# A decoder layer on one core: the front and the projection over blocks of 416 tokens, and two thirds of the modulation made in the mixer

## The reference, cut to what matters

```python
mod = (silu(c) @ w_ada + b_ada)            # 6 x 1024 columns: shift_m, scale_m, gate_m, shift_f, scale_f, gate_f
h = rmsnorm(x, g_pre_mix) * (1 + scale_m) + shift_m
proj = h @ w_in                            # 1536 conv columns, 512 z, 4 b, 4 a, 512 q, 128 k, 128 v
xconv = silu(sum(xp[:, i:i + t] * conv_w[i] for i in range(4)))     # causal, over the 1536 conv columns
o_a = gated delta rule over q, k, v of xconv, chunks of the prompt, state carried; normed, times silu(z)
o_b = sliding-window attention over q_b, k_b, v_b with sinks
x = x + gate_m * rmsnorm(concat(o_a, o_b) @ w_o, g_post_mix)
h = rmsnorm(x, g_pre_ffn) * (1 + scale_f) + shift_f
x = x + gate_f * rmsnorm(square(relu(h @ w_up)) @ w_down, g_post_ffn)
```

## Time and profile before

| | us |
|---|---|
| median of 3 runs (3320.49 to 3322.53) | 3320.68 |
| the profiled execution | 3326.54 |
| its span in the profile | 3324.7 |
| TensorE busy in the span | 3082.3 (93%) |
| VectorE busy | 1573.7 (47%) |
| ScalarE busy | 906.7 (27%) |
| GpSimd busy | 424.6 (13%) |

### The profile page before, as it was taken

The page is one execution under the profiler, slowest core; times in us unless marked ns, Lnnn a source line. Parts: engine busy times, 40 slices in busy tenths (PEclk is TensorE's granted clock), DMA queues, the critical chain, the costliest instruction groups (busy, mean ns, idle before and its releaser), DMA issues. The chain is left out here.

```text
span 3324.7 us, 53221 instructions
## 1 busy us (share of the span) xinstructions
PE 3082.3 (93%) x20508; PEld 2771.5 (83%) x20508; DVE 1573.7 (47%) x2062; ACT 906.7 (27%) x1675; POOL 424.6 (13%) x573
## 2 busy tenths in 40 slices
PE   6799999978999999778987999999998999999996
PEld 2399999977888888767877889988997899999995
DVE  1373655724555555534543444344445444444444
ACT  2332333332333333312333111111212212122121
POOL 2011111112333333100110000000003100000003
PEclk9899999987999999957998999999999999999998
DMA  6643434340111121133544101111114311111112
GB/s 228 220 123 116 137 113 138 114 134 22 50 53 50 53 59 50 41 88 115 179 139 118 51 25 50 50 44 32 50 51 138 94 45 31 50 50 50 50 51 101
DMA packets 320081, 278.92 MB, mean 84 GB/s; under 512 B 13402, under 2 KB 291135, under 8 KB 319960
## 3 DMA queue, kind: packets, MB, share of 16 engines
q1 hardware_dynamic: 312408, 252.58, 25.7%
q0 software_dynamic: 7568, 24.91, 2.0%
HBM read 216.23 MB, written 62.16 MB: 84 GB/s over the span
## 5 line engine op out<-in xcount | busy, mean ns | idle before, releaser
L81 PE MATMUL up_ps<-h_hi,w_up_hi 128*128 128x264 f32 (+1 forms) x2048 | 580.5, 283 | 20.0 <-DVE h_lo L2523 13.2
L82 PE MATMUL up_ps<-h_lo,w_up_hi 128*128 128x264 f32 (+1 forms) x2048 | 583.2, 285 | 0.0
L83 PE MATMUL up_ps<-h_hi,w_up_lo 128*128 128x264 f32 (+1 forms) x2048 | 580.5, 283 | 0.0
L2545 DVE TENSOR_TENSOR y<-y,down_ps 128x1024 f32<-128x1024 f32 (+1 forms) x272 | 332.0, 1220 | 316.0 <-PE down_ps L83 315.4
L81 PE MATMUL down_ps<-w_down_hi,u_hi 128*128 128x512 f32 x1088 | 433.5, 398 | 17.3 <-issue 9.2
L83 PE MATMUL down_ps<-w_down_hi,u_lo 128*128 128x512 f32 x1088 | 429.6, 395 | 0.0
L82 PE MATMUL down_ps<-w_down_lo,u_hi 128*128 128x512 f32 x1088 | 428.0, 393 | 0.0
L81 PEld LDWEIGHTS up_ps<-h_hi,w_up_hi 128*128 128x128 f32 x2048 | 389.2, 190 | 22.7 <-issue 14.5
L81 PE MATMUL proj_ps<-h_hi,w_in_hi 128*128 128x262 f32 x1408 | 400.9, 285 | 0.0
L82 PE MATMUL proj_ps<-h_lo,w_in_hi 128*128 128x262 f32 x1408 | 400.2, 284 | 0.0
L83 PE MATMUL proj_ps<-h_hi,w_in_lo 128*128 128x262 f32 x1408 | 399.3, 284 | 0.0
(11 more groups left out here) (437 smaller groups left out, 4856.3 us busy)
## 6 DMA issues: line engine op xcount, KB each, us to landing
w_in_raw<-in_w_in SPq DMA_DIRECT2D x91, 512.0 KB, 3.9
w_up_raw<-in_w_up SPq DMA_DIRECT2D x66, 512.0 KB
w_down_raw<-in_w_down SPq DMA_DIRECT2D x64, 512.0 KB, 4.6
w_ada_cols<-in_w_ada SPq DMA_DIRECT2D x16, 1536.0 KB, 7.0
proj_scratch<-chunk_out POOLq DMA_DIRECT2D x88, 256.0 KB, 3.3
qkv<-proj_scratch SPq DMA_DIRECT2D x16, 768.0 KB, 5.0
x_tile<-in_x_prompt SPq DMA_DIRECT2D x16, 512.0 KB
mixed_T<-mixed_scratch SPq DMA_DIRECT2D x16, 512.0 KB, 4.4
```

What stands on the lines that cost most here:

```text
L81: nc.tensor.matmul(out, whi, mhi, start=first, stop=False)
L82: nc.tensor.matmul(out, whi, mlo, start=False, stop=False)
L83: return nc.tensor.matmul(out, wlo, mhi, start=False, stop=last)
L2545: v.tensor_tensor(acc, acc, pd[r, (par * H.tiles + t) % 2], ALU.add).then_inc(H.s_y, 1)
```

## The change

The modulation stage makes only the first 2048 of the 6144 columns (shift_m and scale_m): their weights are loaded row-wise, whole, during `constants` (8 DMAs of 1 MB), and TensorE takes them as stationary weights (128x128, unsplit float32) with `scT` as the 9 moving columns, 128 products into one accumulator. During `constants` the first 416 rows of x and the first three chunks of w_in are loaded too. `xnT` is gone.

The projection goes over 5 blocks of 416 tokens (the last one holds 384 of the prompt and the 32 samples), so each product is 416 columns wide and a chunk is 24 products. It norms and turns the next block's x itself: the loads on SyncE, the square on ScalarE, the power on GpSimd, four transposes per k-slice on TensorE after the chunks 12 to 19, and the modulation on VectorE straight from PSUM. The block's left neighbours for the convolution are kept as 3 columns per chunk (`chunk_tails`) instead of being computed again. The first tap is made by ScalarE while it reads PSUM, in a second reading; VectorE makes three. The b and a columns are one position among the others (the seventeenth). Buffers are three deep instead of two, and the loops are written out.

The other 4096 columns are made in the mixer, 256 per period: SyncE loads 1 MB into the unused `w_o_raw`, TensorE makes eight float32 products and two small transposes, VectorE reads both; after the last period VectorE derives what the later stages need. Two scratch tiles of the mixer move into `w_o_raw`, so w_o is loaded after a wait for them.

```diff
+BT = 3 * P + TS
+NBLK = (T + TS) // BT
+SUB = (P, P, P, TS)
 constants, SyncE:
+                for kk in range(KD):
+                    sp.dma_start(k["w_ada_rows"][:, kk, :], io["w_ada"][kk * P:(kk + 1) * P, 0:2 * D]).then_inc(k["w_ada_loaded"][kk], 16)
+                    if kk % 2 == 0:
+                        j = kk // 2
+                        sp.dma_start(k["x_rows"][0:SUB[j], j], io["x"][j * P:j * P + SUB[j], :]).then_inc(k["x_loaded"][j], 16)
+                for c in range(3):
+                    sp.dma_start(k["w_in_raw"][:, c], io["w_in"][:, c * P:(c + 1) * P].rearrange("(k p) n -> p k n", p=P)
+                                 ).then_inc(k["w_in_loaded"][c], 16)
                 sp.wait_ge(s_vec, 16 * (8 + 3 + NS))
 modulation, TensorE:
+                for kk in range(KD):
+                    pe.wait_ge(k["w_ada_loaded"][kk], 16)
+                    for c in range(2 * KD):
+                        last = nc.tensor.matmul(pm[:, c, :], wa[:, kk, c * P:(c + 1) * P], k["scT"][:, kk, :],
+                                                start=False, stop=(kk == KD - 1 and c == 2 * KD - 1))
+                last.then_inc(s_mod, 1)
 projection, TensorE:
+                def chunk(b, i):
+                    n = b * NPOS + i
+                    pe.wait_ge(s_hi, n + 1)
+                    pe.wait_ge(s_lo, n + 1)
+                    after(pe, s_ev, n - R + 1)
+                    for kk in range(KD):
+                        if i == 0:
+                            pe.wait_ge(s_hh, KD * b + kk + 1)
+                            pe.wait_ge(s_hl, KD * b + kk + 1)
+                        last = three_pass(nc, pp[:, n % R, 0:BT], whi[:, n % R, kk, :], wlo[:, n % R, kk, :],
+                                          hhi[:, b % 2, kk, :], hlo[:, b % 2, kk, :], kk == 0, kk == KD - 1)
+                        if n == 0 and kk + 2 < KD:
+                            turn(0, kk + 2)
+                    last.then_inc(s_mm, 1)
...
+                for b in range(NBLK):
+                    for i in range(NPOS):
+                        chunk(b, i)
+                        if b < last_block and 12 <= i < 12 + KD:
+                            turn(b + 1, i - 12)
+                        if i == 18:
+                            turn_ba(b)
 projection, ScalarE:
+                def split(n):
+                    if n < NBLK * NPOS:
+                        act.wait_ge(s_raw[n % R], 16 * (n // R + 1))
+                        after(act, s_mm, n - R + 1)
+                        a.copy(whi[:, n % R], raw[:, n % R]).then_inc(s_hi, 1)
...
+                    else:
+                        a.mul(yb[:, r], pp[:, r, 0:BT], k["taps"][:, 3 * CC + i:3 * CC + i + 1])
+                        a.copy(xb[:, r, CW - 1:], pp[:, r, 0:BT]).then_inc(s_ev, 1)
+
+                def silu(b, i):
+                    q = st_no(b, i) % R
+                    act.wait_ge(s_y, conv_no(b, i) + 1)
+                    a.activation(so[:, q], yb[:, (b * NPOS + i) % R], ACT.Tanh).then_inc(s_th, 1)
...
+                for b in range(NBLK):
+                    for i in range(NPOS):
+                        if b < last_block and 13 <= i < 13 + KD:
+                            slice_hi(b + 1, i - 13)
+                        split(b * NPOS + i + 2)
+                        chunk(b, i)
+                        if b < last_block and i < 12 and i % 3 == 0:
+                            square(b + 1, i // 3)
+                        if kind(i) == "conv":
+                            silu(b, i)
 projection, VectorE:
+                def conv(b, i):
+                    n = b * NPOS + i
+                    r, c = n % R, conv_no(b, i)
+                    dve.wait_ge(s_ev, n + 1)
+                    dve.wait_ge(s_pfx, c + 1)
+                    for tap in range(CW - 1):
...
+                for b in range(NBLK):
+                    for i in range(NPOS):
...
+                        if what == "conv":
+                            conv(b, i)
+                        if ahead and i < 12 and i % 3 == 1:
+                            mean(b + 1, i // 3)
+                        if ahead and 14 <= i < 14 + KD:
+                            slice_lo(b + 1, i - 14)
+                        if ahead and 12 <= i < 12 + KD:
+                            modulate(b + 1, i - 12)
+                        split(b * NPOS + i + 2)
+                        if ahead and i < 12 and i % 3 == 2:
+                            norm(b + 1, i // 3)
+                        if what in SO:
+                            finish(b, i)
 mixer, TensorE:
+                def mod_products(g):
+                    pe.wait_ge(s_mr[g % 2], 16 * (g // 2 + 1))
+                    after(pe, s_oa, g)
+                    for kk in range(KD):
+                        last = mm(b_w[0:9, 0:MC], k["scT"][:, kk, :], mod_raw[g % 2][:, kk, :], start=(kk == 0), stop=(kk == KD - 1))
+                    last.then_inc(s_mp, 1)
...
                     level(level_z, 5)
+                    level(mod_products)
                     attn(attend)
                     level(level_y, 6)
                     prep(level0)
+                    level(mod_turn)
                     level(level_z, 6)
 mixer, VectorE:
                     level(step_x, 5)
+                    level(read_mod)
                     attn(scale_attn)
                     prep(start_x)
+                    level(mod_columns)
                     level(step_x, 6)
```

More of the change, by code:

```diff
@@ L224, in modulation @@
 def modulation(nc, io, k):
-    GC = 3
     with ExitStack() as ctx:
         m = Mem(nc, ctx)
-        xt = m.sb("x_tile", [P, 2, D])
-        xn = m.sb("x_normed", [P, 2, D])
+        xt, wa = k["x_rows"], k["w_ada_rows"]
         sq = m.sb("x_squares", [P, D])
[L232 to L244, removed]
-        s_ss, s_ms, s_rr, s_xn = m.sem("x_sumsq_done"), m.sem("x_meansq_done"), m.sem("x_rrms_done"), m.sem("x_normed_done")
[L246 to L250, removed]
-        with nc.Block() as block:
[L252 to L263, removed]
@@ L265, in _ @@
             @block.scalar
             def _(act):
[L267 to L276, removed]
@@ L411, in projection @@
[L411 to L422 removed]
+        sq = m.sb("x_next_squares", [P, D])
@@ new lines, in projection, with kind, chunk_of, column @@
+        s_pfx, s_keep = m.sem("chunk_prefix_done"), m.sem("chunk_tails_kept")
+        s_bt, s_br = m.sem("ba_turned"), m.sem("ba_read")
+        def kind(i):
+            return "conv" if i < CC else "silu" if i < 16 else "ba" if i == 16 else "plain"
+        def chunk_of(i):
+            return i if i < 16 else i - 1
+        def column(i):
+            return 2048 if i == 16 else chunk_of(i) * P + (2 * HA if i > 16 else 0)
+        def count(b, i, kinds):
+            return b * sum(kind(x) in kinds for x in range(NPOS)) + sum(kind(x) in kinds for x in range(i))
@@ L484, in _, with turn @@
-                with pe.Fori(0, NBLK // 2) as i:
-                    for q2 in range(2):
-                        block_of(i * 2 + q2, q2)
+                def turn(b, kk):
+                    if b > 0:
+                        pe.wait_ge(s_xn, 4 * b)
+                    after(pe, s_h, KD * b + kk - 1)
+                    for j in range(4):
+                        last = nc.tensor.transpose(pt[:, kk % 2, j * P:j * P + SUB[j]], xt[0:SUB[j], j, kk * P:(kk + 1) * P],
+                                                   k["ident"][0:SUB[j], 0:SUB[j]])
+                    last.then_inc(s_xt, 1)
@@ new lines, in _ @@
+                        modulate(0, kk + 1)
+                    slice_lo(0, kk)
+                split(1)
+                for b in range(NBLK):
+                    for i in range(NPOS):
+                        what = kind(i)
+                        ahead = b < last_block
+                        if what == "conv":
[11 more added lines that the diff above has]
+                            finish(b, i)
+                        if i == 19:
+                            read_ba(b)
@@ L657, in projection @@
+                pool.wait_ge(k["pad_stored"], 16)
+                for q in range(R):
+                    pool.wait_ge(s_st[q], 16 * len(range(q, NBLK * NCH, R)))
         m.clear_sems()
```

594 lines of the change are left out of this document (282 added, 312 removed).

## The result

The changed kernel takes 3332.68 us (median of 8 runs, 3329.55 to 3341.54), the kernel before 3320.89 beside it: ratio 1.0035, 95% interval 1.0025 to 1.0045. The forecast was 3318, 2.8 us faster than before, with more chance on faster (0.45) than on no change (0.32) or slower (0.23). So it is slower by about 11.8 us, inside the range of 3285 to 3347, but with the other sign. A second set of runs of the same two kernels gave 1.0034 (1.0023 to 1.0045).

What follows compares the result with a forecast made beforehand. TensorE was taken to bound projection and mixer, being busy nearly throughout. A gain of 61.8 us up to the mixer's start and 59 us more in the mixer gave -2.8, so 3318 us for the median; range 3285 to 3347.

Steps and rivals of the forecast that it cites:

- The baseline: Whole kernel: a difference worked out on the profile's axis (3326.5 us) is taken from the median of 3320.7.
- The first chunk: Projection's start: two slices per round of 4.1 us, 16.5 in all; second chunk starts 17 us in (13 to 19).
- the slower one (0.15): Rival, ScalarE between tanh and next chunk's second read: convolution chunks take 5.3 us, 24 more, 3342 in all; chance 0.15.
- the ring of the convolution chunks: Projection: convolution end, tanh, weight split, two PSUM reads, next convolution; 4.9 us, above TensorE's 4.48.
- Chunks with a convolution: Projection: 59 chunks at 4.9 us, 289 less 0.7 per block for buffers, 285.6; bounds 264 to 313.
- ring of 5.3: Rival in the projection: convolution chunks take 5.3 us each, 24 us more in all, 3342; chance 0.15.
- Turns: Projection on TensorE: each turn of x is four transposes, 0.4 us; 32 cost 12.8, the ba turns 1.5.
- Plain products: Projection: 24 products of 416 columns take 4.48 us a chunk; 55 chunks without convolution cost 246.4.
- the hold: Constants: SyncE's third w_in issue waits behind queued row pieces until 34.6 us; bounds 20 (not held) to 38.
- Modulation: Modulation stage: 128 weight-loading products at 1.2 GHz, 0.4375 us each, 56.0 plus 0.5 for clearing; end at 92.4.
- The rival with a chance of 0.12: Modulation stage: products run at 2.4 GHz, 28 us less there, 3290 in all; chance 0.12.
- Nothing hides them: Mixer: eight products and two transposes per period add 3.7 us, unhidden; 59 us over 16 periods, bounds 53 to 64.

Runs made afterwards that it cites:

- the run with the later loads: Changed kernel with the first three w_in loads issued in the modulation stage instead of the constants; ratio 0.9980 to the kernel before.
- the run without columns: Changed kernel without the mixer's loads, products, turns and reads for the 4096 modulation columns, which are set to zero; ratio 0.9852 to the kernel before.
- the run with the moving form: Changed kernel with the first 2048 modulation columns made by 32 products with 512 w_ada columns moving, then 16 transposes; ratio 0.9967 to the kernel before.

## Why the prediction was wrong, step by step

- **The baseline.** I took a difference on the profile's axis from the median. Both profiles of before lie 5.1 to 5.8 above it, the profile of after lies on its own median. That is 5.6 of the miss of 14.7 us. The median itself was a low one: in three later sets the kernel before had 3323.2, 3324.9 and 3325.5. What the difference of the two levels consists of is open (above); that the mixer's start can move by 7 us from one execution to the next is shown.
- **The first chunk: the failed step.** I let two slices share one round of 4.1 us, 16.5 in all. The low half of a slice stands on VectorE behind the modulation of the next slice, so one slice took one round, 3.65, and the chunk 28.5 instead of 17, far outside my bounds of 13 to 19. These 11.5 us are nearly the whole 11.8 by which the kernel is slower. Changing that order alone gave back 8.7 (up to 1.3 of them by the earlier clock) and left a chunk of 19.3. I had listed the engines that a slice passes through and not the order in which VectorE takes its two steps. No rival of mine had this place: the slower one (0.15) put its loss into the ring of the convolution chunks, which was not the cause.
- **Chunks with a convolution: ring mis-sized.** I added 4.9 from rows of 512 columns: 2.27 for the convolution and 0.27 of handovers. Measured are 2.03 (three steps without idle time between them, from the earlier trace rows I had 0.16 each) and 0.03 to 0.07, 4.50 together. The 59 chunks took 270.9 instead of 285.6, 4.59 each, so TensorE's 4.53 nearly set the pace. The rival "ring of 5.3" was far off; with one more step the mechanism is there (5.12).
- **Turns mis-sized.** A turn took 0.71, and 0.5 more at the first of a block, where VectorE's norm is late (0.38 of it is TensorE's wait); the 0.4 was half of the eight back-to-back transposes of the earlier trace rows, which all have 128 rows, while a turn's fourth has 32 and costs some 0.15 us more, and the product behind a turn 0.11 more. With the ba turns they cost 26.7 (170.8 for the 32 chunks with turns, 105.0 for the 23 other plain ones, less 55 x 4.53), not 14.3.
- **Plain products.** 4.53 a chunk and not 4.48, 2.8 over the 55. These three terms cancel (-14.7, +12.4, +2.8), which is why 546.3 was forecast and 546.9 measured for the rest of the projection. A right sum of wrong terms, by luck.
- **Constants.** Right: the hold was real and ended at 36.4 (34.6 forecast, though its own terms give 34.8 to 35.4), and the run with the later loads shows that it cost 17.3. When it ended, all rows of w_ada and x and 616 of the 3,072 w_in rows had landed, so 1,432 pieces stood ahead of the third load, near the forecast's 1,500.
- **Modulation.** Right for this form: 54.6 against 56.0, at half speed. The rival with a chance of 0.12 would have needed the other form.
- **Mixer.** Right: 3.74 a period (3.7), 59.8 over sixteen, none hidden; the run without columns confirms it. The 55.2 of the two profiles is less because the profile of before had the later clock at its start: 673.2 us for the mixer, where the run without columns took 667.7 for the same work; the changed kernel's own profile was some 1 us above its usual 727.3. "Nothing hides them" was true of the place, not of the work: 1.74 of each period's 3.74 can be hidden.
- **After the projection** the mixer follows after 13.6 us (12.2 forecast), and the later stages moved by 0.2.

The miss of 14.7 us is then, up to 0.1 of rounding: 5.6 baseline, -0.9 start of the projection, 11.5 first chunk, 0.6 rest of the projection, 1.4 behind it, -3.8 mixer, 0.2 later.

## What to carry to other kernels

List for each engine the order of its steps before pricing a pipeline round: a step that sits behind another one's wait makes a chain out of a ring, and swapping two lines undoes it. Work put into an engine's wait gains only if its own reader is not in the queue that caused the wait. Where issues can be held, as here, loads for a later stage belong behind the barrier and not ahead of it; and small differences need the same kernel profiled more than once.

## What the runs showed of the hardware

- The clock column reads 1.00 from 37 to 123 us in the changed kernel, but the trace holds no clock record before 125.6, the first. The durations tell: a 416-column product took 0.55 us there, as in the stretch of 0.50 of the run with the moving form, and 0.35 later. So ahead of the first record 1.00 means "unknown".
- Unsplit float32 products of 128x128 weights with 9 moving columns kept TensorE busy from 37.9 to 92.6 at 0.427 us each, the pace of 1.2 GHz (0.44 at 0.50 granted and 0.23 at 1.00 for one moving column); the same sums with 512 columns moving had 2.4 GHz 2.9 us after the first product.
- Issuing three 0.5 MB loads of 512-byte rows behind 10 MB held SyncE until 36.4 or 37.1 us, whether the issue began at 14.2 (22.1 us) or at 19.6 (17.5 us). At these moments 1,432 and 1,185 pieces stood ahead of the last load. In the kernel before a held issue ended at 24.85 with 1,516 ahead of it.
- Float32 transposes of 128 rows between long products start 0.11 us apart; one of 32 rows behind them starts 0.20 after the last and holds the next product for 0.17, both at 2.4 GHz granted. Four of them (three and one) cost 0.71 in place, 0.11 of it in the product behind, and pairing two such groups saved 0.06.
- The kernel's tail moves as its start does: behind the mixer's last load issue the same code took 1917.8 to 1924.2 us in fourteen profiles, the longest where the clock was low longest (204 us).
